# A four-layer attention and gating trunk: residual with features on the partitions, weight units cast two events behind their load, mixing products on half of the array's columns

## The reference

```python
D_MODEL, BATCH, SEQ, DEPTH = 2048, 4, 8192, 4
HEAD_DIM, N_Q_HEADS, N_KV_HEADS, WINDOW, CHUNK = 64, 16, 4, 128, 128
for l in range(DEPTH):
    h = _rmsnorm(x, norm_g[l])                       # over the 2048 features
    proj = einsum('bsd,de->bse', h, w_in[l])         # 2048 -> 5632
    q, k, v, g_a, z_u, z_v, g_b = split(proj)        # 1024 256 256 1024 1024 1024 1024
    q = _rmsnorm(q per head, q_norm[l]); k = _rmsnorm(k per head, k_norm[l])
    attn = sliding_window_128(q, k, v, sinks[l], alibi) * silu(g_a)
    z_u = gelu(z_u); z_v = gelu(z_v)
    # per chunk of 128 positions, one 128x128 causal matrix for each of 16 heads of 64 channels
    sgu = z_u * (tril(w_s[l]) @ z_v + b_s[l]) * silu(g_b)
    x = x + concat([attn, sgu]) @ w_out[l]           # 2048 -> 2048
```

## Time and profile before

| | |
|---|---|
| runs shown | 7987.17, 8267.01, 8987.27 us (median 8267.01) |
| profiled execution | 7963.68 us, of which the slowest core's span is 7962.0 us |
| spans of the eight cores | 7927.1 to 7962.0 us |
| TensorE busy | 7752.7 us, 97% |
| ScalarE, VectorE, GpSimd busy | 3153.9, 2864.1, 645.4 us |
| DMA | 1925.05 MB, 242 GB/s over the span |

### The profile page before, as it was taken

How to read it: one execution, slowest core, us unless ns; L and a number is a source line. 1 busy time by engine, 2 the same in 40 slices (tenths; PEclk the granted TensorE clock), 3 DMA queues, 4 the chain that set the end, 5 groups by cost and what they waited for, 6 DMA issues and landing times.

```text
span 7962.0 us, 140270 instructions; the slowest of 8 cores (7927.1 to 7962.0 us)
## 1 busy us (share of the span) xinstructions
PE 7752.7 (97%) x51494; PEld 4698.3 (59%) x51494; DVE 2864.1 (36%) x4126; ACT 3153.9 (40%) x5272; POOL 645.4 (8%) x622
## 2 busy tenths in 40 slices
PE   5899999999999999999999999999999999999999
PEld 3456555556666655666566665556666666665555
DVE  2523333433333334323333333344323433233333
ACT  1334444433333344434443344444433443233332
POOL 0000000000000000000000000000000000000000
PEclk8999999999999999999999999999999999999999
DMA  9988877786776777887876678777886665555554
GB/s 271 305 279 266 263 252 248 253 253 239 244 249 233 249 250 251 267 282 257 256 256 228 239 255 266 245 251 247 273 257 222 222 229 198 205 188 201 185 181 159
DMA packets 394284, 1925.05 MB, mean 242 GB/s; under 512 B 33680, under 2 KB 37904, under 8 KB 202768
## 3 DMA queue, kind: packets, MB, share of 16 engines
q1 hardware_dynamic: 346640, 1815.92, 69.1%
q10 hardware_dynamic: 46976, 100.17, 3.5%
HBM read 1650.68 MB, written 265.29 MB: 241 GB/s over the span
## 4 chain that ended last, share of the span: by engine, by line
PE 89%; DMA 5%; ACT 2%; SPq 1%; DVE 1%; issue 1%; ACTq 0%; DVEq 0%; POOL 0%
PE pp L283 87%; PE pp L286 2%; SPq L289 1%; DMA m_wslot<-scr 1%; DMA m_cst<-w_in 1%; DMA m_cst<-w_out 1%; ACT m_hb L274 1%; DVE m_qs L274 1%; DVE m_hb L274 0%; DMA m_xs<-x 0%; ACT m_sqf L274 0%; ACT m_cb L274 0%; ACTq L289 0%; DMA m_xr<-w_in 0%; DMA m_wslot<-w_out 0%
## 5 line engine op out<-in xcount | busy, mean ns | idle before, releaser
L283 PE MATMUL pp<-m_hT,m_wslot 128*128 128x512 bf16 (+1 forms) x13824 | 2849.1, 365 | 55.8 <-ACT m_ex L274 17.5
L283 PE MATMUL pp<-m_wslot,m_hT 128*128 128x256 bf16 x21344 | 2373.3, 273 | 37.8 <-DVE m_wslot L274 24.2
L283 PEld LDWEIGHTS pp<-m_wslot,m_hT 128*128 128x128 bf16 x21344 | 2089.6, 98 | 292.0 <-issue 40.3
L283 PEld LDWEIGHTS pp<-m_hT,m_wslot 128*128 128x128 bf16 x13824 | 1351.1, 98 | 1422.5 <-issue 115.2
L274 DVE TENSOR_TENSOR m_tf<-pp,m_bias 64x512 f32<-64x512 f32 (+1 forms) x576 | 373.0, 648 | 2303.7 <-PE pp L283 2239.1
L274 DVE TENSOR_TENSOR m_xr<-m_xr,pp 128x512 f32<-128x512 f32 x1064 | 705.2, 680 | 1009.9 <-PE pp L283 1008.2
L283 PE MATMUL pp<-m_wslot,m_zu 128*128 128x512 bf16 x4256 | 968.1, 381 | 19.8 <-DVE m_xr L274 19.6
L283 PE MATMUL pp<-m_wslot,m_ga 128*128 128x512 bf16 x4256 | 955.2, 381 | 8.6 <-DMA m_wslot<-scr 4.6
L283 PEld LDWEIGHTS pp<-m_wslot,m_zu 128*128 128x128 bf16 x4256 | 395.4, 98 | 574.1 <-issue 137.6
L283 PEld LDWEIGHTS pp<-m_wslot,m_ga 128*128 128x128 bf16 x4256 | 409.6, 98 | 491.9 <-issue 42.9
L274 POOL TENSOR_TENSOR m_zu<-m_tf,m_gbs 128x512 bf16<-128x512 f32 (+1 forms) x288 | 312.0, 1083 | 3737.0 <-DVE m_tf L274 3359.9
(11 more groups left out here) (49 smaller groups left out, 3451.5 us busy)
## 6 DMA issues: line engine op xcount, KB each, us to landing
m_wslot<-scr SPq DMA_DIRECT2D x1054, 1024.0 KB, 8.9
m_cst<-w_in SPq DMA_DIRECT2D x147, 1024.0 KB, 15.4
x_scr<-m_xr SPq DMA_DIRECT2D x100, 1024.0 KB, 17.6
m_xs<-x_scr SPq DMA_DIRECT2D x100, 1024.0 KB, 6.6
m_xr<-x_scr SPq DMA_DIRECT2D x99, 1024.0 KB, 10.0
scr<-m_cb ACTq DMA_DIRECT2D x180, 512.0 KB, 9.8
m_xr<-x SPq DMA_DIRECT2D x33, 1024.0 KB, 17.3
out<-m_xr SPq DMA_DIRECT2D x33, 1024.0 KB, 10.3
```

What stands on the lines that cost most here:

```text
L283: S.op("pe", lambda e: e.matmul(out, lhsT=lhsT, rhs=rhs, start=start, stop=stop), reads=reads, writes=writes)
```

## The change

The input, the residual in memory and the output hold features on the partitions: a block is 128 x 2048, with 16 chunks of 128 features side by side, each with the block's 128 positions.

- **Norm.** No transposes. `norm_chunk` multiplies one chunk (128 features by all positions of the tile) with the gain, now one scalar for each partition (`gT`), and with `rB`, the inverse root broadcast to all partitions, straight into `hT`. It stands behind each G_OA slot. `xs` is loaded in quarters of a tile (four chunks), each after the quarter two before it is used.
- **Sum of squares.** In the `zu` and `zv` groups of the next tile ScalarE squares the finished residual (`last_squares`, two chunks a group) and VectorE adds them up in `acc`; `split_sums` writes the sum as two bf16 halves; `total` is two products with a matrix of ones; the result goes to memory as `rs` and comes back broadcast for the next layer (`load_rstd`). In layer 0 the input's squares are made in the `ga` groups from a load of their own (`first_squares`), so each quarter of its tiles is loaded twice; its first five blocks go through `norm_block`.
- **Output slots.** A slot is one chunk of 128 output features by all positions, with the weights as the stationary side. A tile has 16 slots a half, whether it has three or four blocks. Between attention units stand now one, two or three slots (`sizes`), with two more behind the last; the first G_OA group takes the first half of the contraction for four banks, then the second half.
- **Mixing.** After both column chunks of a `gb` group, each head's product runs alone with 64 stationary columns and its own half of the PSUM partitions: 8 products of 128 columns a chunk where there were 4 of 256, and one bias addition of 128 partitions where there were two of 64.
- **Units.** A unit's cast stands two events behind its load; its load now takes the buffer that the cast just ahead of it frees.

```diff
+            more = conv["k"] < len(conv["list"])
+            if len(conv["loaded"]) > (1 if more else 0):
+                conv_cast()
+            if more:
...
+                conv["loaded"].append((l, unit, k))
...
+                    xu += [(l, b0, nb, q) for q in range(4)] * (2 if l == 0 else 1)
...
+        def split_sums(w):
+
+            OP("dve", "tensor_copy", [Bacc], [Bhl], out=hl[:, 0, 0:w], in_=acc[:, 0:w])
+            TT("dve", [Bacc, Bhl], [Bhl], out=hl[:, 1, 0:w], in0=acc[:, 0:w], in1=hl[:, 0, 0:w], op=ALU.subtract)
+
+        def total(w):
+            b = nextbank()
+            for part in range(2):
+                MM([Bones, Bhl], [PB[b]], bank(b)[:, 0:w], ones_bf[:, :], hl[:, part, 0:w], part == 0, part == 1)
+            return b
...
+        def add_square(c, w, nb, src, reads):
+
+            if c == 0:
+                ACT(reads, [Bacc], out=acc[:, 0:w].rearrange("p (n t) -> p n t", n=nb), in_=src, func=AF.Square)
...
+            sq = sqf[:, 512 * h:512 * h + w]
+            ACT(reads, [Bsqf[h]], out=sq.rearrange("p (n t) -> p n t", n=nb), in_=src, func=AF.Square)
+            TT("dve", [Bacc, Bsqf[h]], [Bacc], out=acc[:, 0:w], in0=acc[:, 0:w], in1=sq, op=ADD)
...
+        def norm_chunk(c):
+
+            if c % 4 == 0:
+                cur["u"], cur["x"] = xs_take()
+            u, (l, b0, nb, q) = cur["u"], cur["x"]
+            w = nb * 128
+            OP("dve", "scalar_tensor_tensor", [Bxs[u], BgT, BrB], [BhT[c]], out=hT[:, c, 0:w].rearrange("p (n t) -> p n t", n=nb),
+               in0=chunk(u, nb, c % 4), scalar=gT[:, 16 * l + c:16 * l + c + 1],
+               in1=rB[:, 0:w].rearrange("p (n t) -> p n t", n=nb), op0=MUL, op1=MUL)
+            if c % 4 == 3:
+                xs_load()
+
...
+            def last_squares(k):
+
+                if pend:
+                    pnb = pend[0][2]
+                    for c in (2 * k, 2 * k + 1):
+                        add_square(c, pnb * 128, pnb, xr[:, 0:pnb, c * 128:c * 128 + 128], [Bxc[c]] + Bxr[0:pnb])
...
+                us = []
+                for cc in range(2):
+                    b = proj_B(s, cc, nb)
+                    u = turn("g")
+                    us.append(u)
+                    ACT([PB[b]], [Bgbs[u]], out=gbs[u][:, 0:cols], in_=bank(b)[:, 0:cols], func=AF.Silu)
                 for cc in range(2):
                     j = 2 * g + cc
-                    b = proj_B(s, cc, nb)
-                    u = turn("g")
-                    ACT([PB[b]], [Bgbs[u]], out=gbs[u][:, 0:cols], in_=bank(b)[:, 0:cols], func=AF.Silu)
-                    bp = nextpair()
-                    pv = pp[bp // 2][:, :].rearrange("p (n f) -> p n f", n=4)
+                    b = nextbank()
                     for n in range(nb):
-                        MM([Bz[2 * n + j // 4], BwsT], [PB[bp + n // 2]], pv[:, n, :], zv[:, n, j * 128:(j + 1) * 128],
-                           wsT[:, 2 * j:2 * j + 2, :], True, True)
+                        for half in range(2):
+                            c0 = j * 128 + 64 * half
+                            MM([Bz[2 * n + j // 4], BwsT], [PB[b]], bank(b)[64 * half:64 * half + 64, n * 128:n * 128 + 128],
+                               zv[:, n, c0:c0 + 64], wsT[:, 2 * j + half, :], True, True)
+                    u = us[cc]
                     u2 = turn("t")
-                    for half in range(2):
-                        rows = slice(64 * half, 64 * half + 64)
-                        TT("dve", [PB[bp], PB[bp + 1], Bbias], [Btf[u2]],
-                           out=tf[u2][rows, 0:cols].rearrange("p (n t) -> p n t", n=nb),
-                           in0=pv[rows, 0:nb, half * 128:half * 128 + 128],
-                           in1=bias[rows, j, :].unsqueeze(1).to_broadcast([64, nb, 128]), op=ADD)
+                    TT("dve", [PB[b], Bbias], [Btf[u2]], out=tf[u2][:, 0:cols].rearrange("p (n t) -> p n t", n=nb),
+                       in0=bank(b)[:, 0:cols].rearrange("p (n t) -> p n t", n=nb),
+                       in1=bias[:, j, :].unsqueeze(1).to_broadcast([128, nb, 128]), op=ADD)
                     TT("dve", [Btf[u2], Bzu[j]], [Btf[u2]], out=tf[u2][:, 0:cols], in0=tf[u2][:, 0:cols], in1=zu[:, j, 0:cols], op=MUL)
                     TT("pool", [Btf[u2], Bgbs[u]], [Bzu[j]], out=zu[:, j, 0:cols], in0=tf[u2][:, 0:cols], in1=gbs[u][:, 0:cols], op=MUL)
 
+            if pend:
+                split_sums(pend[0][2] * 128)
...
+                pl, pb0, pnb = pend.pop()
+                rstd(total(pnb * 128), 1, pnb * 128, rrow[0:1, 0:pnb * 128], Brr)
+                DMA("rs", [Brr], Brs[pb0:pb0 + pnb], out=A["rs"][pl:pl + 1, pb0 * 128:(pb0 + pnb) * 128], in_=rrow[0:1, 0:pnb * 128])
...
+            if nxt is not None and nxt[0] > 0:
+                load_rstd(nxt[0], nxt[2], nxt[3], 0)
+                if last["layer_end"] and nxt[0] < NH:
+                    load_rstd(nxt[0], nxt[2] - 1, 1, 384)
...
+            def out_slots(base, src, bsrc, final):
                 for q in range(4):
                     s = next_w()
                     w = wslot[s][:, :].rearrange("p (e n) -> p e n", e=8)
-                    for n in range(nb):
-                        b = nextbank()
-                        for e in range(8):
-                            MM([Bws[s], bsrc(e, n)], [PB[b]], bank(b), src[:, e, n * 128:(n + 1) * 128], w[:, e, :], e == 0, e == 7)
-                        xo = xr[n][:, 512 * q:512 * q + 512]
-                        TT("dve", [PB[b], Bxr[n]], [Bxr[n]], out=xo, in0=xo, in1=bank(b), op=ADD)
+                    banks = [nextbank() for _ in range(4)] if final and q == 0 else [None] * 4
+
+                    def part(dc, es):
+                        for e in es:
+                            MM([Bws[s]] + bsrc(e), [PB[banks[dc]]], bank(banks[dc])[:, 0:cols], w[:, e, dc * 128:dc * 128 + 128],
+                               src[:, e, 0:cols], e == 0, e == 7)
+
+                    if final and q == 0:
+                        for dc in range(4):
+                            part(dc, range(4))
+                    for dc in range(4):
+                        c = 4 * q + dc
+                        if banks[dc] is None:
+                            banks[dc] = nextbank()
+                        part(dc, range(4, 8) if final and q == 0 else range(8))
+                        xo = xr[:, 0:nb, c * 128:c * 128 + 128]
+                        TT("dve", [PB[banks[dc]], Bxc[c]] + Bxr[0:nb], [Bxc[c]], out=xo, in0=xo,
+                           in1=bank(banks[dc])[:, 0:cols].rearrange("p (n t) -> p n t", n=nb), op=ADD)
...
+            gaps = len(units) - 1
+            sizes = [2] + [(k + 1) * 12 // gaps - k * 12 // gaps for k in range(gaps)] + [2]
+
+            def some_slots(k, step):
+                for r in range(sizes[k]):
                     next(os_slots)
-                    if step is not None:
-                        step(k)
-
-            two_slots(unit_E(1, unit_S(1)))
+                    if step is not None and r == 0:
+                        step(0)
...
+            for i, _ in enumerate(out_slots(G_OA, ga, lambda e: Bga[e // 4][0:nb], True)):
+                if rest is not None and i == 0:
+                    mix_matrices(*rest)
+                if key_block and i == 3:
+                    keys = mini(l + 1)
+                if key_block and i == 5:
+                    keys()
+                while nxt is not None and done * (16 - begin) < 16 * (i + 1 - begin):
+                    norm_chunk(done)
                     done += 1
...
```

More of the change, by code:

```diff
@@ L246, in _main @@
         Bx = [B("x%d" % i) for i in range(NH + NOWN)]
+        Brs = [B("rs%d" % i) for i in range(NH + NOWN)]
         Bscr = {}
@@ L544, in prep_c @@
[L544 to L557 removed]
+                xu.append((l, tiles[0][0] - 1, 1, None))
@@ new lines, in _main, with xs_load @@
+            for ti, (b0, nb) in enumerate(tiles):
+                if l == 0 and ti == 0:
+                    xu += [(l, b0 + n, 1, None) for n in range(nb)]
+                else:
+                    xu += [(l, b0, nb, q) for q in range(4)] * (2 if l == 0 else 1)
+        xp = {"load": 0, "use": 0}
+        def xs_load():
+            k = xp["load"]
+            if k >= len(xu):
+                return
+            xp["load"] += 1
+            l, b0, nb, q = xu[k]
+            u = k % 2
+            eng = "act" if 2 <= k < 7 else "sp"
+            if q is None:
+                DMA("xs%d" % u, [Bx[b0]], [Bxs[u]], eng=eng, out=xs[u][:, :], in_=xsrc(l)[b0])
+            else:
+                DMA("xs%d" % u, Bx[b0:b0 + nb], [Bxs[u]], eng=eng, out=xs[u][:, 0:nb * 512].rearrange("p (n f) -> p n f", n=nb),
+                    in_=xsrc(l)[b0:b0 + nb, :, 512 * q:512 * q + 512].rearrange("n p f -> p n f"))
@@ L559, in layer_bias, with first_squares @@
+        def first_squares(q):
+            u, (l, b0, nb, _) = xs_take()
+            for i in range(4):
+                add_square(4 * q + i, nb * 128, nb, chunk(u, nb, i), [Bxs[u]])
+            xs_load()
```

(3 more changed lines are left out.)

244 lines of the change are left out of this document (112 added, 132 removed).

## The result

The changed kernel is slower, by less than 2%: 1.0116 times the time of before (95% interval 1.0097 to 1.0136). Its medians are 8474.42 us against 8299.15 us, its best executions 8075.15 and 8075.28 us against 7984.72 and 7986.23 us. Before: 7972.0, 7976.3 and 7956.4 us on the three chips used. After: 8059.8 us, **+88**; the forecast was -46.

What follows compares the result with a forecast made beforehand. TensorE, busy 97% of the slowest core's span, was taken as the bound. Terms -117 + 2 - 30 + 15 + 51 + 36 + 12 - 20 + 5 = -46 us took 7963.7 to 7918 us; range 7800 to 8045, leaving out two in ten.

Steps and rivals of the forecast that it cites:

- Transposes, mixing and slots: TensorE products: transposes gone -117 us, mixing in 64-column products -30 us, output slots with more products +2 us.
- The pairing of 64-column products: Mixing: two 64-column products run side by side, 0.63 us a group, -30 us; rival without pairing 7975 us, chance 0.10.
- The attention gaps: Attention phase: sum products behind one-slot gaps wait 0.8 us for the value bank, some 80 times; +51 us, 0 to 75.
- Late weights: Conversion tiles: two more 1 MB loads in the G_OA groups delay weight slots, 2 us a tile; +36 us, bounds 0 and 90.
- Layer 0's second loads: Layer 0, in the rival "late weights decide": 4 MB a tile find no free time, 7 tiles, 90 us.
- late weights decide: Rival, conversion tiles: the 6.4 us arrive in full (90 instead of 36), layer 0's second loads add 90; 8062 us, chance 0.16.
- Start: First stretch to 400 us: 3 MB more loads cost 10 us, spread casts free staging earlier; +5 us (-15 to +25).
- Waits removed: TensorE's waits on Exp and `qn`: later casts no longer wait for loads, `prep_b` leaves query groups; -20 us (0 to -26).
- `norm_chunk`: G_OA slots: 1.3 us of VectorE work hides in each 1.73 us slot; price 0.
- `xs` late: Rival, tile boundaries: a late `xs` transfer makes `norm_chunk` hold VectorE, 36 tiles x 3 us; 8025 us, chance 0.06.
- Layer 0's squares beside attention: Layer 0, turn from `ga` to attention: squares, sums and root where ScalarE is nearly full; +12 us (0 to 25).

Runs made afterwards that it cites:

- run 4: Changed kernel with the two quarter loads of `xs` behind G_OA chunks 11 and 15 moved to the next tile's query groups 0 and 2: 7979.7 us, +8 against before.
- run 7: Kernel before with only the mixing products changed to eight of 64 stationary columns a chunk: 7944.1 us, -32, ratio 0.9969.
- run 6: Changed kernel without layer 0's second loads, squares taken of whatever stands in `xs`: 8051.4 us, +75 against the kernel before.
- run 10: Changed kernel with `norm_block` squaring in one bf16 activation, summed by 16 ones products: 8034.5 us, +78 against the kernel before.
- run 3: Changed kernel with each unit cast one event behind its load again: 8023.7 us, +52 against the kernel before.
- run 8: Kernel before with only the unit casts moved to two events behind their load: 7966.4 us, -10, ratio 0.9995.
- run 12: run 8 with one pending cast made ahead of the attention phase in a layer's last tile: 7936.0 us, -20 against the kernel before, ratio 0.9976.
- run 11: Changed kernel with attention slots shared out otherwise, one unit fewer followed by a single slot: 8036.1 us, +80 against the kernel before.
- run 5: Changed kernel with four edits together, those of run 3, run 4, run 10 and other slot sizes as in run 11: 7928.0 us, -48 against the kernel before.
- run 9: Changed kernel with the two loads behind G_OA chunks 11 and 15 left in place but issued on ScalarE's queue: 8019.0 us, +63 against the kernel before.

## Why the prediction was wrong

**What held.** Transposes, mixing and slots change TensorE's busy time by -117 - 30 + 2 + 15 = -130 us. Run 4 has the same products, and its core 1 is at 7618.9 us of busy time against 7752.7, -134 us:

```profile
PE 7618.9 (96%) x51183; PEld 4597.3 (58%) x51183; DVE 3207.1 (41%) x5053; ACT 2894.2 (37%) x5112; POOL 681.4 (9%) x657
```

The pairing of 64-column products, the term that I had to choose, is confirmed by 0.56 us a group and by run 7 (-32, forecast -30). Sixteen products in pairs at 0.056 us are 0.45 us, so both changes of shape together cost 0.11, not 0.19. The Trainium skill (TensorEngine Tiling (Array Packing), Key Properties and Restrictions) says that column tiling turns fast weight loading off; if so, it costs nothing here, since the loads of a pair don't set the pace. The attention gaps are confirmed in mechanism, place and size: 0.67 us at the gap shown, 44.6 us in 89 places (0.8, 51 and some 80), 0.50 us each on average. ScalarE and VectorE hold no group of `zu`, and ScalarE's waits for units, 217 us before, are gone. The last layer's four-block tile falls by 2.2 to 2.8 us where my terms add up to 3.6 + 1.0 - 0.43 - 1.6 = 2.6.

**Late weights, +36 us, is the step that failed most.** The mechanism and the turn of the tile as its place were right, and the bound of 90 held; the value did not. Run 4 gives back 80 us when 2 MB a tile leave the end of G_OA. I made two errors. I let 3 of the 6.4 us be absorbed by the half phase at a DMA share of 0.60. But the two loads stand at the end of the phase, behind that free time, in front of stores and the fullest groups: in the windows above the share is at 0.99 or more for four stretches running. And I counted the wait itself only. TensorE's clock is lower behind it, as shown below.

**Layer 0's second loads** are no part of it: the rival "late weights decide" named 8062 us, close to the 8060 measured, yet 90 of its added us were for those loads, and run 6 prices them at 13 at most. Its other half, the peak paid in full, is what run 4 shows. The number was hit by luck, by a sum with one wrong term and without the losses that follow here.

**Start, +5 us (-15 to +25), measured +27 to +31.** I counted the bytes of this stretch and not the chain: in `norm_block` ScalarE, GpSimd, VectorE, TensorE, ScalarE and VectorE follow one another, 16.1 us a block for four blocks, against 8.4. The queue, full before at a share of 1.00 from 50 to 100 us, isn't even full there now (core 3, columns as in the earlier trace rows):

```profile
50.00:100.00 50.00, 1.11 (x6) 0.41 (x6) 18.04 (x60) 8.10 (x12) 17.81 (x24) 0.54 0.72 244
```

That a queue is full before a change says nothing of the stage when the change puts a longer chain into it. Run 10 gives back 23 to 30 us.

**Waits removed, -20 us,** came as -16 in the rows, and brought a cost that I had looked at and put at nothing: I wrote that the load held back by its cast has nothing due behind it. Run 3 prices the later casts at 36 us. At a layer's end the load held back is that of `w_s`, due at once: 12 us in the changed kernel, 26 in run 8, 5 in run 12, against 3.5 in the kernel before. Nor were the waits I started from complete: with all rows TensorE waited 63 us from 400 us on, not some 50.

**`norm_chunk`.** I took its price as 0. It is 13.5 us of waits for `m_hT` on core 3, 26.9 in run 4 on core 0, 34.3 on core 0 of run 6: on core 3 VectorE waits 72 us in 42 places for the quarter loads of `xs`, at most 6.9 us. This is the rival "`xs` late", as a small loss rather than 3 us a tile. Layer 0's squares beside attention (+12) could not be told apart from it.

**The end, put at nothing, is +6 us:** the last stores wait for the last slot, as shown above.

**The sum.** To -46 come +44 for late weights, +22 to +26 for the start, +4 for the waits removed, +36 for the later casts, +6 for the end and +13 to +34 for `m_hT`: 79 to 104 us, where 88 were measured. Taken the other way the parts overlap: from +88 less 80 (run 4), 36 (run 3), 23 to 30 (run 10) and 8 to 24 (run 11) is -59 to -82, and run 5, with all four, measures -48. Its end (+6) and its waits for `m_hT` (1.6 to 25.0 us on cores 4 to 7) are left in it; the rest is not assigned.

**What stays open.** Why one core of each two neighbours (0 and 1, 2 and 3, and so on) loses 25 to 48 us more than the other in tiles 9 to 16 (run 6: 1722 us on core 0, 1674 on core 1). Over the whole span the two lie 25 to 89 us apart in all twelve dies counted for the changed kernel, some 70 in the middle, against 22 before, and which of them is the slower changes between executions. The mean of a die's cores rises by 61 us where its slowest rises by 88, so 27 of the 88 us are a wider spread between cores. The DMA packets of this stretch, changed kernel (core 3) and kernel before (core 5):

```profile
DMA packets 100282, 428.60 MB, mean 256 GB/s; under 512 B 7101, under 2 KB 7361, under 8 KB 62117
```

```profile
DMA packets 87218, 426.29 MB, mean 252 GB/s; under 512 B 6927, under 2 KB 6927, under 8 KB 45154
```

The same bytes move in more and smaller packets, since `xs` comes in quarters; whether that is the reason was not tried. How run 3's 36 us come about, beyond the 7 to 10 of `w_s`, is open too.

## What to carry to other kernels

A full queue is paid by what stands behind it, not where it fills: read the DMA share in stretches as short as one group, and ask of each moved load whether the free time lies ahead of it or behind it. Where cores differ, look at the slowest, not at one. Where a buffer is held one step longer, look for the one load, at the end of a loop, whose reader comes at once. In a stage that starts up, follow one item through all engines and add up the chain before counting bytes.

## What was not expected of the hardware

**Most waits cost more than their length.** TensorE in order of time (changed kernel, core 3), and windows of the products at 1453 and 1462 us:

```profile
737.75 7.15 PE L286 MATMUL pp<-m_wslot,m_hT 128*128 128x256 bf16 x64 [2.92 <-DMA m_wslot<-scr]
...
973.46 16.85 PE L286 MATMUL pp<-m_wslot,m_hT 128*128 128x256 bf16 x128 [5.25 <-DMA m_wslot<-scr]
...
1453.13 7.15 PE L286 MATMUL pp<-m_wslot,m_hT 128*128 128x256 bf16 x64 [1.65 <-DMA m_wslot<-scr]
1462.46 8.81 PE L286 MATMUL pp<-m_wslot,m_hT 128*128 128x256 bf16 x64 [2.19 <-DMA m_wslot<-scr]
1471.12 7.07 PE L286 MATMUL pp<-m_hT,m_wslot 128*128 128x512 bf16 x32
```

```profile
1453.00:1460.20 7.20, 7.07 (x64) 6.18 (x64) 2.77 (x4) 3.73 (x6) 0.00 (x0) 1.00 1.03 284
1462.40:1471.30 8.90, 8.84 (x65) 7.26 (x66) 1.00 (x2) 0.03 (x1) 0.00 (x0) 0.81 1.00 305
```

After the wait of 2.19 us the same 64 products take 8.81 us instead of 7.15, at a mean granted clock of 0.81, which is a part of the time at 1.2 instead of 2.4 GHz. 128 products take 14.14 us where nothing is late (at 1675 us); behind the 6.22 us wait they take 15.96, behind the one of 5.25 us 16.85. Not every wait does it: behind 2.92 us (at 737.75) and behind 1.65 us 64 products take their 7.15 us. Ten waits of more than 2 us in layer 0 of core 3 are 44 us of waiting; behind nine of them the products take 1.4 to 2.7 us longer by their starts, some 17 us in all.

**A transfer on another queue is in the way too.** With 2 MB a turn on ScalarE's queue the weights on SyncE's still landed up to 27.5 us after their issue (run 9).
